# First loads reordered, blank products on TensorE at the start, and the first output tile in two transfers

## The chip, the core and the metric

The kernel runs on one NeuronCore of a Trainium2 chip. The metric is the device time of one execution in microseconds (us). A profile of one execution shows when each engine works: PE is TensorE (its weight loads are listed as PEld), DVE is VectorE, ACT is ScalarE, POOL is GpSimd, and SP only issues transfers. An issue of a transfer is listed as SPq or ACTq.

## The reference, cut to what matters

Two transformer blocks are computed for 256 tokens of width 1024, in float32. Only the first lines and the last one touch this change:

```python
# first block, start: normalise x, project it with w_in
hn = rmsnorm(h, norm_mix_g[l])
proj = jnp.einsum('bsd,de->bse', hn, w_in[l])
...
# attention of two kinds, gated FFN, then a second block with three more stages
...
# the end: the last down projection of the FFN is added to h, then normalised
h = h + swiglu(rms_norm(h, norm_ffn[layer]), ffn_w13[layer], ffn_w2[layer])
...
return rms_norm(h, final_norm)
```

## The kernel before, in words

The 256 tokens are two tiles (t = 0 and 1) of 128 tokens, one token to a partition. The width 1024 is eight chunks of 128 features. Every large product is made of three: each float32 operand is split into a high part in the type fp32r and the remainder as a low part, and PE computes high x high, low x high and high x low.

Weights come in "granules", mostly 1 MB each, through a ring of three buffers (`raw`, `w_hi`, `w_lo`). SP loads a granule into `raw`, ACT copies it to `w_hi` (line 548, for the first granule lines 624 and 627, a half each), DVE subtracts to get `w_lo` (line 1090, for the first granule line 1188, twice), and PE multiplies. Each engine has its own list of instructions, written out by hand in the order in which it executes them. Semaphores tie the lists together.

The start, engine by engine:

- SP issues x tile 0 and x tile 1 (line 400), then the first half of granule 0 of `w_in` (line 405, semaphore `first_in`), then its second half (line 406), then granules 1 and 2 (line 388), then four small transfers.
- ACT issues the identity matrix (`const`, line 613), the gain of the first norm (`norm_mix_g`, line 614) and three small vectors. It then copies the turned gain to `vcol` (line 620), converts the first half of granule 0 (line 624), then four kinds of work in turn: chunks 2 and 3 of x to `x_hi` (line 559), the second half of granule 0 (line 627), chunks 4 to 7 of x, and granule 1.
- PE waits for the identity, does two products identity x identity (`keep_busy`, line 1948, the result is not used), turns x tile 0 (line 1953, eight transposes), turns the gain (line 1979), turns x tile 1, and does two more unused products. A transpose of x tile 1 with c odd raises `xt_done`: both tiles of two chunks are then turned.
- DVE waits for `vcol` and the first `xt_done`. It writes chunks 0 and 1 of `x_hi` (line 1193), the low parts of chunks 0 to 3 (line 1102), the low parts of both halves of granule 0 (line 1188), and the low parts of chunks 4 to 7.
- PE's first real products (`first_product(0, 0)`, line 1997) need the first half of `w_hi` and the chunks of x as they come; the products with `w_lo` (line 2002) need both calls of line 1188. `first_product(1, 4)` does the same for granule 1.

The end, after the last products:

- DVE adds the product to h in four quarters (`add_last`, line 1793). ACT squares each quarter and sums it (lines 1071 and 1075, each followed by a read of the sum). DVE makes the variance (lines 1797 and 1799), POOL the inverse root (line 438), and then ACT scales the left half of a tile (`scale_half`, line 1067) and DVE the right half (`finish`, line 1808).
- Between the squares of tile 1's left half and its right half, ACT does `scale_half(0)`.
- SP sends tile 0 to `out` in one transfer after both its halves (line 424), then tile 1's right half (line 426). ACT sends tile 1's left half (line 1078).

Of the kernel before, what the change touches and what calls it, by code (L numbers as in the profile page):

```python
# [25 lines left out]
P = 128  # L26
S = 256
TT = S // P
D = 1024
# [33 lines left out]
V_MIX1, V_LB, V_CQ, V_CKV, V_END = 0, 8, 24, 26, 27  # L63
# [116 lines left out]
def build(nc, a, out):  # L180
# [9 lines left out]
    with ExitStack() as ctx:  # L190
# [10 lines left out]
        h = sb("h", [P, TT, D])  # L201
        xn = sb("xn", [P, TT, D])
# [8 lines left out]
        ps = ctx.enter_context(nc.psum_tensor("ps", [P, 8, 512], F32))  # L211
        bias_scratch = nc.dram_tensor("bias_scratch", (COPIES, HEADS, BIAS_LEN), F32, kind="Internal").ap()

        ident = const[:, K_ID:K_ID + P]


        def region(start, *dims, parts=P):
# [31 lines left out]
        bias_row = xn[0:HEADS, 1, 0:BIAS_LEN]  # L249

# [53 lines left out]
            setup warmed vrow_T vcol_done taps_T taps_done bias_ps bias_sb trig_ready  # L304
# [65 lines left out]
        def _(sp):  # L370
# [19 lines left out]
            def load_ffn(n0):  # L390
                for n in range(n0, n0 + 5):
                    load(n)
                with sp.Fori(0, 3) as i:
                    for j in range(6):
                        load(n0 + 5 + j, i, "columns" if j % 3 < 2 else "rows")
                for n in range(n0 + 23, n0 + 33):
                    load(n)

            for t in range(TT):
                sp.dma_start(h[:, t, :], a["x"][0, P * t:P * t + P, :]).then_inc(x_in[t], 16)  # L400

# [3 lines left out]
            sp.dma_start(dst[:, 0:2, :], first[:, 0:2, c0:c0 + cols]).then_inc(s["first_in"], 16)  # L405
            sp.dma_start(dst[:, 2:4, :], first[:, 2:4, c0:c0 + cols]).then_inc(raw_in[0], 16)
# [14 lines left out]
            load_ffn(G["ffn2"])  # L421
            sp.wait_ge(s["out_a"], 1)
            sp.wait_ge(s["out_b"], 1)
            sp.dma_start(out[0, 0:P, :], h[:, 0, :]).then_inc(s["out_done"], 16)
            sp.wait_ge(s["out_b"], 2)
            sp.dma_start(out[0, P:S, 512:D], h[:, 1, 512:D]).then_inc(s["out_done"], 16)
            sp.wait_ge(s["out_done"], 48)
# [110 lines left out]
        def _(act):  # L538
# [73 lines left out]
            act.activation(stat[:, 158:159], minus_half[:, 0:1], ACT.Square).then_inc(s["warmed"], 1)  # L612
            act.dma_start(const[:, K_ID:K_ID + P], a["const"][:, K_ID:K_ID + P]).then_inc(s["const_in"], 16)
            act.dma_start(vrow[V_MIX1:V_MIX1 + 8, 0, :], a["norm_mix_g"].rearrange("l (c p) -> (l c) p", p=P)).then_inc(s["mix_in"], 16)
# [6 lines left out]
            act.wait_ge(s["vcol_done"], 1)  # L621
            first_cols = 2 * granules[0][5]
            act.wait_ge(s["first_in"], 16)
            act.activation(w_hi[:, 0, 0:first_cols], raw[:, 0, 0:first_cols], ACT.Copy).then_inc(s["first_hi"], 1)
            first_operand_hi(2, 4)
# [443 lines left out]
            for t in range(TT):  # L1069
                act.wait_ge(s["last_added"], 2 * t + 1)  # L1070
                act.activation(xn[:, t, 0:512], h[:, t, 0:512], ACT.Square, accum_out=ssq_half[:, t:t + 1]).then_inc(s["half_ready"], 1)
                if t == 1:
                    scale_half(0)
                act.wait_ge(s["last_added"], 2 * t + 2)
                act.activation(xn[:, t, 512:D], h[:, t, 512:D], ACT.Square, accum_out=ssq[:, 16 + t:17 + t]).then_inc(s["ssq_ready"], 1)
            scale_half(1)
# [5 lines left out]
        def _(dve):  # L1082
# [97 lines left out]

            dve.memset(minus_half, -0.5).then_inc(s["setup"], 1)
# [643 lines left out]
        def _(pe):  # L1825
# [119 lines left out]
            def keep_busy(bank, count):  # L1945

                for _ in range(count):
                    pe.matmul(ps[:, bank, 0:P], ident, ident, start=True, stop=True)
# [25 lines left out]

            pe.wait_ge(s["const_in"], 16)
            keep_busy(7, 2)
            turn_x(0)
            pe.wait_ge(s["mix_in"], 16)
            pe.transpose(ps[:, 4, 0:8], vrow[0:8, 0, :], ident[0:8, 0:8]).then_inc(s["vrow_T"], 1)
            turn_x(1)  # L1980
            keep_busy(7, 2)
# [515 lines left out]
```

## Time and profile before

| what | value |
|---|---|
| median of three runs | 1000.36 us |
| the three runs | 999.68, 1000.36, 1000.6 us |
| the profiled execution, its own time | 999.73 us |
| span of the profiled execution, first to last instruction | 997.9 us |
| PE busy in the span | 981.6 us (98%) |
| DVE, ACT busy in the span | 677.7 us, 542.8 us |
| granted TensorE clock, mean over the span | 0.998 |

The span is 1.8 us shorter than the profiled execution's own time; what lies around it is outside the profile. The times in the rows below count from the start of the span.

### The profile page before, as it was taken

How to read it: one execution, taken by the hardware profiler on the slowest of the kernel's cores; microseconds unless marked ns; L12 is line 12 of the kernel's file. 1: busy time of each engine (PE TensorE's matmuls, PEld its weight loads, DVE VectorE, ACT ScalarE, POOL GpSimd, SP SyncE). 2: the span in 40 equal slices, each digit the busy share in tenths (PEclk: the TensorE clock that was granted, in tenths of full speed). 3: DMA queues.
4: the chain of work that ended last, by engine and by line, in shares of the span. 5: the costliest groups of instructions: out<-in, count | busy, mean ns of one | idle time of the engine just before them, and what ended most of it. 6: DMA issues, size and time to landing. Idle time of an engine off the chain costs nothing.

```text
span 997.9 us, 15646 instructions
## 1 busy us (share of the span) xinstructions
PE 981.6 (98%) x6349; PEld 841.6 (84%) x6349; DVE 677.7 (68%) x831; ACT 542.8 (54%) x708; POOL 42.9 (4%) x68
## 2 busy tenths in 40 slices
PE   7999999999999999999999999999999999999997
PEld 6887777898888888887889888888899898888885
DVE  5689787688777787777767565656656566555564
ACT  6676664476555565634445444444555455444452
POOL 1210000000000005000000000000000000000000
PEclk9999999999999999999999999999999999999999
DMA  8354335466656555844347565656553446656541
GB/s 306 103 192 158 109 120 178 161 211 211 209 170 209 171 168 164 261 146 155 120 133 259 188 207 190 204 185 201 185 168 133 155 142 214 207 172 207 174 163 43
DMA packets 121283, 175.89 MB, mean 176 GB/s; under 512 B 3167, under 2 KB 89770, under 8 KB 121226
## 3 DMA queue, kind: packets, MB, share of 16 engines
q1 hardware_dynamic: 118860, 168.82, 51.0%
q0 software_dynamic: 1600, 5.09, 1.6%
q10 hardware_dynamic: 766, 1.16, 0.5%
q8 instruction: 42, 0.69, 0.3%
q14 instruction: 15, 0.12, 0.0%
HBM read 173.82 MB, written 1.25 MB: 175 GB/s over the span
## 4 chain that ended last, share of the span: by engine, by line
PE 76%; issue 19%; DVE 2%; DMA 1%; ACT 1%; POOL 1%; SPq 0%; POOLq 0%; DVEq 0%; ACTq 0%
PE ps L1851 22%; PE ps L1901 16%; PE ps L1872 10%; PE ps L1900 7%; PE ps L1888 5%; PE ps L1915 3%; PE ps L1923 2%; DMA raw<-in_w_in 1%; PE ps L2141 1%; PE ps L2336 1%; PE ps L1903 1%; PE ps L1966 1%; PE ps L2169 1%; PE ps L2397 1%; PE ps L1997 1%
## 5 line engine op out<-in xcount | busy, mean ns | idle before, releaser
L1090 DVE TENSOR_TENSOR w_lo<-raw,w_hi 128x2048 fp32r<-128x2048 f32 (+3 forms) x153 | 345.3, 2261 | 125.2 <-ACT w_hi L548 124.9
L1901 PE MATMUL ps<-x_both,w_hi 128*128 128x512 f32 x992 | 342.7, 396 | 0.0
L548 ACT ACTIVATE w_hi<-raw 128x2048 fp32r<-128x2048 f32 (+3 forms) x161 | 302.4, 1879 | 58.9 <-PE ps L1851 40.1
L1900 PE MATMUL ps<-x_both,w_lo 128*128 128x256 f32 x868 | 242.0, 279 | 0.0
L1901 PEld LDWEIGHTS ps<-x_both,w_hi 128*128 128x128 f32 x992 | 179.1, 188 | 34.5
L1900 PEld LDWEIGHTS ps<-x_both,w_lo 128*128 128x128 f32 x868 | 163.6, 189 | 5.5
L803 ACT ACTIVATE work<-ps 128x512 f32<-128x512 f32 x66 | 39.3, 596 | 150.2 <-PE ps L1901 134.4
L1851 PE MATMUL ps<-w_hi,x_both 128*128 128x512 f32 (+1 forms) x320 | 101.5, 387 | 0.3 <-DVE w_lo L1090 0.3
L1851 PE MATMUL ps<-w_hi,hid_hi 128*128 128x512 f32 x240 | 93.8, 391 | 0.0
L1851 PE MATMUL ps<-w_hi,hid_lo 128*128 128x512 f32 x240 | 93.4, 389 | 0.0
L1851 PE MATMUL ps<-w_lo,hid_hi 128*128 128x512 f32 x240 | 93.4, 389 | 0.0
L1498 DVE TENSOR_TENSOR work<-ps,work 128x512 f32<-128x512 f32 x66 | 45.5, 689 | 63.1 <-ACT work L803 62.8
L1872 PE MATMUL ps<-w_hi,x_both 128*128 128x512 f32 x256 | 84.3, 398 | 0.1
L1851 PEld LDWEIGHTS ps<-w_hi,x_both 128*128 128x128 f32 x320 | 59.2, 188 | 13.0 <-issue 1.9
L1851 PE MATMUL ps<-w_lo,x_both 128*128 128x512 f32 (+1 forms) x160 | 60.7, 379 | 0.0
L837 ACT ACTIVATE hid_hi<-work 128x512 fp32r<-128x512 f32 x33 | 20.8, 631 | 68.9 <-DVE work L1530 62.7
L1872 PEld LDWEIGHTS ps<-w_hi,x_both 128*128 128x128 f32 x256 | 48.1, 188 | 10.4 <-DVE w_lo L1090 0.5
L1851 PEld LDWEIGHTS ps<-w_hi,hid_lo 128*128 128x128 f32 x240 | 45.0, 188 | 9.5
L1851 PEld LDWEIGHTS ps<-w_lo,hid_hi 128*128 128x128 f32 x240 | 45.1, 188 | 9.4
L1851 PEld LDWEIGHTS ps<-w_hi,hid_hi 128*128 128x128 f32 x240 | 45.1, 188 | 8.2
L1915 PE MATMUL ps<-x_both,w_hi 128*128 128x256 f32 x384 | 49.4, 284 | 1.5 <-DVE x_both L1109 1.5
L1872 PE MATMUL ps<-w_lo,x_both 128*128 128x512 f32 x128 | 49.9, 390 | 0.0
(294 smaller groups left out, 1274.2 us busy)
## 6 DMA issues: line engine op xcount, KB each, us to landing
raw<-in_ffn_w SPq DMA_DIRECT2D x66, 1024.0 KB, 5.1
raw<-in_w_up SPq DMA_DIRECT2D x22, 1024.0 KB, 5.1
raw<-in_hgrn_w_in SPq DMA_DIRECT2D x16, 1024.0 KB, 5.5
raw<-in_w_in SPq DMA_DIRECT2D x12, 1024.0 KB, 5.2
raw<-in_moba_w_in SPq DMA_DIRECT2D x12, 1024.0 KB, 5.2
raw<-in_w_down SPq DMA_DIRECT2D x11, 1024.0 KB, 5.0
raw<-in_w_out SPq DMA_DIRECT2D x4, 1024.0 KB, 5.1
raw<-in_hgrn_w_out SPq DMA_DIRECT2D x4, 1024.0 KB, 5.7
```

The costliest lines, as they stand in the source:

```text
L548: act.activation(w_hi[:, n % RING, 0:kc * cols], raw[:, n % RING, 0:kc * cols], ACT.Copy).then_inc(s["hi_ready"], 1)
L803: act.activation(up[:, p % 2, 2 * half:2 * half + 2, :], src[:, :, S:2 * S], ACT.Copy).then_inc(s["up_half"], 1)
L837: act.activation(hid_hi[:, 2 * par:2 * par + 2, :].rearrange("p a b -> p (a b)"), hid[:, par, :], ACT.Copy).then_inc(s["hhi_ready"], 1)
L1090: dve.tensor_tensor(w_lo[:, n % RING, sl], raw[:, n % RING, sl], f32(w_hi[:, n % RING, sl]), ALU.subtract).then_inc(s["lo_ready"], 1)
L1498: dve.tensor_tensor(v, src[:, :, 0:S], v, ALU.add).then_inc(s["up_taken"], 1)
L1851: ins = pe.matmul(ps[:, bank + 2 * c + t, 0:n_c], x[:, chunks + kk, P * t:P * t + P], w[:, n % RING, w0:w0 + n_c], start=(first and kk == ...
L1872: ins = pe.matmul(ps[:, bank + 2 * c + t, :], x[:, chunks + kk, P * t:P * t + P], w[:, n % RING, w0:w0 + 512], start=(first and kk == 0 an ...
L1888: ins = pe.matmul(ps[:, bank, S * f:S * f + S], w[:, n % RING, 256 * k + P * f:256 * k + P * f + P], x[:, k, :], start=(k == 0 and q == 0) ...
L1900: pe.matmul(out[:, 0, :], w_lo[:, n % RING, at], x_hi[:, k, :], start=False, stop=False)
L1901: ins = pe.matmul(out, w_hi[:, n % RING, at], x_both[:, k, :, :], start=(k == 0), stop=(k == DC - 1))
L1915: pe.matmul(out[:, :, at_t], w_hi[:, n % RING, 256 * k + P * f:256 * k + P * f + P], x_both[:, k, :, at_t], start=(k == 0 and t == 0), sto ...
L1923: ins = pe.matmul(ps[:, banks[f], 0:S], w_lo[:, n % RING, 256 * k + P * f:256 * k + P * f + P], x_hi[:, k, :], start=False, stop=(k == DC ...
```

## The change

Five edits, all at the two ends of the kernel:

1. SP loads x tile 1 after the first half of granule 0 and no longer ahead of it.
2. ACT issues the gain ahead of the identity. Its wait for its own `vcol` comes after the conversion of granule 0's first half.
3. DVE first writes zeros into 128 columns of `xn` (`blank`), and PE multiplies this blank with itself eight times as its first work. PE then waits for identity and gain, turns the gain ahead of x tile 0, and does four unused products identity x identity between the two tiles of x. The two after x tile 1 stay.
4. ACT's `scale_half(0)` comes after both squares of tile 1.
5. SP sends the right half of tile 0 as soon as it is scaled, and the left half in a second transfer.

```diff
--- before.py
+++ after.py
@@ -247,6 +247,7 @@
         pool_tmp = region(13776, 4, 160 * TT)
         g_ik = region(16592, HD)
         bias_row = xn[0:HEADS, 1, 0:BIAS_LEN]
+        blank = xn[:, 0, 0:P]
 
 
         conv = region(0, 2, 4, S)
@@ -301,7 +302,7 @@
         table = sb("table", [NBUCKET + 1, HEADS])
 
         names = """small_in mix_in first_in first_hi first_lo gate_scale first_x taps_in pos_in posrow_in const_in shapes_in gain_in table_in masks_in final_in final2_in bias_out bias_in out_done
-            setup warmed vrow_T vcol_done taps_T taps_done bias_ps bias_sb trig_ready
+            setup blank warmed vrow_T vcol_done taps_T taps_done bias_ps bias_sb trig_ready
             hi_ready lo_ready products_done
             ssq_ready var_ready rstd_ready  xt_done xhi_ready xlo_ready h_added scaled_done h_final last_added half_scaled half_ready out_a out_b
             row_ready half_turned half_hi half_lo grow_in last_gate og_part og_scaled f_half f_sum q_half q_sum
@@ -396,13 +397,16 @@
                 for n in range(n0 + 23, n0 + 33):
                     load(n)
 
-            for t in range(TT):
+            def load_x(t):
                 sp.dma_start(h[:, t, :], a["x"][0, P * t:P * t + P, :]).then_inc(x_in[t], 16)
+
+            load_x(0)
 
             first = a["w_in"][0].rearrange("(c p) n -> p c n", p=P)
             dst, cols = granule_views(0)
             c0 = granules[0][4]
             sp.dma_start(dst[:, 0:2, :], first[:, 0:2, c0:c0 + cols]).then_inc(s["first_in"], 16)
+            load_x(1)
             sp.dma_start(dst[:, 2:4, :], first[:, 2:4, c0:c0 + cols]).then_inc(raw_in[0], 16)
             for n in range(1, RING):
                 load(n)
@@ -419,12 +423,13 @@
             for n in range(G["mq"], G["ffn2"]):
                 load(n)
             load_ffn(G["ffn2"])
+            sp.wait_ge(s["out_b"], 1)
+            sp.dma_start(out[0, 0:P, 512:D], h[:, 0, 512:D]).then_inc(s["out_done"], 16)
             sp.wait_ge(s["out_a"], 1)
-            sp.wait_ge(s["out_b"], 1)
-            sp.dma_start(out[0, 0:P, :], h[:, 0, :]).then_inc(s["out_done"], 16)
+            sp.dma_start(out[0, 0:P, 0:512], h[:, 0, 0:512]).then_inc(s["out_done"], 16)
             sp.wait_ge(s["out_b"], 2)
             sp.dma_start(out[0, P:S, 512:D], h[:, 1, 512:D]).then_inc(s["out_done"], 16)
-            sp.wait_ge(s["out_done"], 48)
+            sp.wait_ge(s["out_done"], 64)
 
 
         @block.gpsimd
@@ -610,18 +615,18 @@
 
             act.wait_ge(s["setup"], 1)
             act.activation(stat[:, 158:159], minus_half[:, 0:1], ACT.Square).then_inc(s["warmed"], 1)
+            act.dma_start(vrow[V_MIX1:V_MIX1 + 8, 0, :], a["norm_mix_g"].rearrange("l (c p) -> (l c) p", p=P)).then_inc(s["mix_in"], 16)
             act.dma_start(const[:, K_ID:K_ID + P], a["const"][:, K_ID:K_ID + P]).then_inc(s["const_in"], 16)
-            act.dma_start(vrow[V_MIX1:V_MIX1 + 8, 0, :], a["norm_mix_g"].rearrange("l (c p) -> (l c) p", p=P)).then_inc(s["mix_in"], 16)
             for r, name in ((V_LB, "hgrn_lb_logits_2"), (V_CQ, "q_a_norm_g"), (V_CKV, "kv_a_norm_g")):
                 v = a[name]
                 v = v.rearrange("l (c p) -> (l c) p", p=P)
                 act.dma_start(vrow[r:r + v.shape[0], 0, :], v).then_inc(s["small_in"], 16)
             act.wait_ge(s["vrow_T"], 1)
             act.activation(vcol[:, 0, 0:8], ps[:, 4, 0:8], ACT.Copy).then_inc(s["vcol_done"], 1)
-            act.wait_ge(s["vcol_done"], 1)
             first_cols = 2 * granules[0][5]
             act.wait_ge(s["first_in"], 16)
             act.activation(w_hi[:, 0, 0:first_cols], raw[:, 0, 0:first_cols], ACT.Copy).then_inc(s["first_hi"], 1)
+            act.wait_ge(s["vcol_done"], 1)
             first_operand_hi(2, 4)
             act.wait_ge(raw_in[0], 16)
             act.activation(w_hi[:, 0, first_cols:2 * first_cols], raw[:, 0, first_cols:2 * first_cols], ACT.Copy).then_inc(s["hi_ready"], 1)
@@ -1069,10 +1074,9 @@
             for t in range(TT):
                 act.wait_ge(s["last_added"], 2 * t + 1)
                 act.activation(xn[:, t, 0:512], h[:, t, 0:512], ACT.Square, accum_out=ssq_half[:, t:t + 1]).then_inc(s["half_ready"], 1)
-                if t == 1:
-                    scale_half(0)
                 act.wait_ge(s["last_added"], 2 * t + 2)
                 act.activation(xn[:, t, 512:D], h[:, t, 512:D], ACT.Square, accum_out=ssq[:, 16 + t:17 + t]).then_inc(s["ssq_ready"], 1)
+            scale_half(0)
             scale_half(1)
             act.wait_ge(s["out_a"], 2)
             act.dma_start(out[0, P:S, 0:512], h[:, 1, 0:512]).then_inc(s["out_done"], 16)
@@ -1178,6 +1182,7 @@
                         add(t, c, 4 + 2 * c + t)
                 return adds
 
+            dve.memset(blank, 0.0).then_inc(s["blank"], 1)
             dve.memset(minus_half, -0.5).then_inc(s["setup"], 1)
             dve.memset(table[NBUCKET:NBUCKET + 1, :], -FAR).then_inc(s["setup"], 1)
             first_cols = 2 * granules[0][5]
@@ -1942,10 +1947,10 @@
                     feature_high(n + g, banks[g], 1, ready if g == 0 else None)
                     feature_low(n + g, banks[g])
 
-            def keep_busy(bank, count):
+            def keep_busy(bank, count, operand):
 
                 for _ in range(count):
-                    pe.matmul(ps[:, bank, 0:P], ident, ident, start=True, stop=True)
+                    pe.matmul(ps[:, bank, 0:P], operand, operand, start=True, stop=True)
 
             def turn_x(t):
                 pe.wait_ge(x_in[t], 16)
@@ -1972,13 +1977,15 @@
                         pe.wait_ge(s["half_lo"], step(k, t, c // 4))
                 return ready
 
+            pe.wait_ge(s["blank"], 1)
+            keep_busy(7, 8, blank)
             pe.wait_ge(s["const_in"], 16)
-            keep_busy(7, 2)
-            turn_x(0)
             pe.wait_ge(s["mix_in"], 16)
             pe.transpose(ps[:, 4, 0:8], vrow[0:8, 0, :], ident[0:8, 0:8]).then_inc(s["vrow_T"], 1)
+            turn_x(0)
+            keep_busy(7, 4, ident)
             turn_x(1)
-            keep_busy(7, 2)
+            keep_busy(7, 2, ident)
             def in_block(b, k):
                 token_product(2 * b + k, 4 * k, 4 + 2 * (b % 2), k == 0, k == 1)
```

## Rows read from the trace of the kernel before

**Rows 1.** The page: busy time, share of the span and instructions of each engine.

```profile
PE 981.6 (98%) x6349; PEld 841.6 (84%) x6349; DVE 677.7 (68%) x831; ACT 542.8 (54%) x708; POOL 42.9 (4%) x68
```

**Rows 2.** Busy time by stretch, PE alone: stretch, length, PE busy, granted clock, DMA share, GB/s.

```profile
20.97:984.00 963.03, 958.89 (x6247) 1.00 0.53 175
991.07:997.93 6.86, 0.00 (x0) 0.74 0.39 153
```

**Rows 3.** The chain that ended last, 0 to 25 us: start, length, what.

```profile
1.20 0.42 SPq L400
...
1.66 7.11 DMA raw<-in_w_in
...
8.86 1.02 ACT w_hi L624
...
9.93 3.82 PE ps L1997 x16
...
15.79 3.58 PE ps L1997 x16
```

**Rows 4.** Timeline of PE's weight loads: start, length, instructions, idle before and releaser.

```profile
4.87 0.93 PEld L1948 LDWEIGHTS ps<-const 128*128 128x128 f32 x4 [4.87 <-DMA const<-in_const]
5.68 1.72 PEld L1953 LDWEIGHTS ps<-const,h 128*128 128x128 f32 x8
...
7.93 0.86 PEld L1953 LDWEIGHTS ps<-const,h 128*128 128x128 f32 x8
...
13.74 1.63 PEld L2002 LDWEIGHTS ps<-w_lo,x_both 128*128 128x128 f32 x8 [0.40 <-DVE w_lo L1188]
```

**Rows 5.** DMA issues of the first 3 us: size and us from issue to landing.

```profile
const<-in_const ACTq DMA_DIRECT2D x1, 64.0 KB, 3.9
...
h<-in_x SPq DMA_DIRECT2D x1, 512.0 KB, 4.9
raw<-in_w_in SPq DMA_DIRECT2D x1, 488.0 KB, 7.1
...
raw<-in_w_in SPq DMA_DIRECT2D x1, 488.0 KB, 7.8
```

**Rows 6.** DMA queues from 5.5 to 7 us: packets, MB, share of 16 engines.

```profile
q0 software_dynamic: 32, 0.00, 41.4%
```

**Rows 7.** Timeline of the start, DVE.

```profile
8.50 0.88 DVE L1193 TENSOR_SCALAR x_both<-ps,vcol 128x256 fp32r<-128x256 f32 x2 [7.49 <-PE ps L1953]
...
10.64 0.88 DVE L1102 SCALAR_TENSOR_TENSOR x_both<-ps,vcol,x_both 128x256 fp32r<-128x256 f32 x2 [0.49 <-ACT x_both L559]
11.44 2.25 DVE L1188 TENSOR_TENSOR w_lo<-raw,w_hi 128x976 fp32r<-128x976 f32 x2
```

**Rows 8.** Timeline of the start, transfers issued by ACT and SP.

```profile
1.36 0.57 ACTq L614 DMA_DIRECT2D work<-in_norm_mix_g  x1
...
2.13 0.68 SPq L406 DMA_DIRECT2D raw<-in_w_in  x1
```

**Rows 9.** Timeline of the end, after the last product.

```profile
991.21 0.68 DVE L1793 TENSOR_TENSOR h<-ps,h 128x512 f32<-128x512 f32 x1
991.73 0.72 ACT L1067 ACTIVATE h<-work,stat 128x512 f32<-128x512 f32 x1 [0.54 <-POOL stat L438]
...
992.36 0.61 ACT L1075 ACTIVATE xn<-h 128x512 f32<-128x512 f32 x1
...
992.88 0.19 ACT L1075 ACTIVATION_READ_ACCUMULATOR xn<-h 128x1 f32 x1
993.17 0.16 DVE L1799 SCALAR_TENSOR_TENSOR stat<-stat 128x1 f32<-128x1 f32 x1 [0.55 <-ACT xn L1075]
993.40 0.55 POOL L438 TENSOR_TENSOR stat<-stat 128x1 f32<-128x1 f32 x1 [1.71 <-DVE stat L1799]
...
993.99 0.75 DVE L1808 SCALAR_TENSOR_TENSOR h<-h,stat,g_final 128x512 f32<-128x512 f32 x1 [0.66 <-POOL stat L438]
...
994.77 0.36 SPq L426 DMA_DIRECT2D out<-h  x1
```

**Rows 10.** The tile out, its three transfers: us from issue to landing.

```profile
DMA to landing us min/median/max: 2.6/2.6/2.8
```

## The prediction

> **What bounds the kernel now.** I read the page's busy times first. PE is busy 981.6 us [rows 1] of a span of 997.9 us, so only 16.3 us are left in which PE does nothing. The busy times by stretch show where they are: between 20.97 and 984.00 PE lacks 963.03 - 958.89 = 4.1 us [rows 2], and after its last product at 991.07 come 6.86 us without it. The rest is the start: 4.87 us before the first product and about half a microsecond before 9.93. The change edits nothing between 21 and 991 us. It can move the time by what it does to the moment at which PE gets through granule 0, and by what it does to the 6.86 us of the end. A measurement of this kernel can tell about 0.2%, 2.0 us, from no change.
>
> The chain of waits shows what releases the first real product: the transfer of granule 0's first half, issued at 1.66 and 7.11 us on its way (1.66 + 7.11 = 8.77), then its conversion from 8.86 for 1.02 us, then the products at 9.93 [rows 3]. The reader should also see the next piece: these 16 products take 3.82 us, the same 16 for granule 1 take 3.58 (0.224 each). The difference of 0.24 us is a second wait: PE's loads of `w_lo` begin at 13.74 after 0.40 idle, released by DVE's line 1188 [rows 4]. So a second chain ends almost with the first, and it is DVE's: it begins at 8.50 when the second tile of x has been turned, holds one wait of 0.49 us (for ACT's chunks 2 and 3), and ends at 11.44 + 2.25 = 13.69 [rows 7]. Without the wait it is 13.69 - 8.50 - 0.49 = 4.70 us of work. Whatever the change does to the first chain, PE cannot leave granule 0 before the second has ended.
>
> **Edit 1, the order of the loads.** x tile 1 was issued at 1.20 [rows 3] and landed 4.9 us later [rows 5], at 6.1; the half granule behind it landed at 8.77. The two swap places in one queue and are nearly of one size (512 and 488 KB). The half granule should land near 6.1 and its conversion end near 7.2, 2.7 us earlier than now. x tile 1 then lands in the place of the half granule. Call that moment T1. Bounds: not before 6.1 plus the time of 488 KB at about 400 GB/s (the spacing of two later 488 KB landings, 8.77 and 2.13 + 7.8 = 9.93 [rows 5, 8], is 1.16 us), so 7.3; and not much after the landing now in that place, 8.8, with 9.1 as outer end. What speaks for the late end is the stretch from 5.5 to 7 us, in which GpSimd's small transfers hold 41.4% of the 16 DMA engines while moving next to nothing [rows 6]. They are issued when they were, so what is in flight then is slowed, and that is now x tile 1. I take 8.7.
>
> Now DVE's chain starts from T1. PE turned tile 1 from 7.93 [rows 4] and DVE began at 8.50, 0.57 later. With T1 = 8.7 DVE begins at 9.27. The wait of 0.49 goes away: ACT has long converted the first half granule and is free for chunks 2 and 3 at once. DVE ends at 9.27 + 4.70 = 13.97, PE starts `w_lo` 0.05 later as now, at 14.02 against 13.74: 0.28 us lost. PE's own side is earlier: eight transposes of x tile 1 (1.1 us) and four passes of unused products (0.43) let it start at about 10.2, and 16 products of 0.224 end at 13.8. The start of real products moves back by about 0.3 as well, though its old releaser, the half granule, came 2.7 us sooner. In this sum the transfer moved ahead buys nothing, because the one moved behind now ends both chains. By T1's bounds the term is 7.3 + 5.32 - 13.74 = -1.1 us to 9.1 + 5.32 - 13.74 = +0.7 us. At the low end the second half of granule 0 (landing 9.93, conversion 1.02, then eight products of 0.224 after it: 12.8) limits it to -0.9.
>
> **Edit 2, gain ahead of identity.** The gain's issue takes 0.57 us [rows 8] and the zeroing ahead about 0.1 (bounds 0.05 and 0.5, by a 128-partition copy of 256 columns, half of 0.88 us in [rows 7]), so the identity, which takes 3.9 us from issue [rows 5] and starts PE at 4.87 [rows 4], lands about 0.65 us later, near 5.5. Turning the gain and x tile 0 takes about 0.2 + 0.86 at the fast pitch or 0.2 + 1.72 at the slow one [rows 4]: done by 7.5 at the latest, over a microsecond before T1. The cover is the wait for x tile 1. If x tile 1 came at 7.3, the slow case would cost 0.2 us.
>
> **Edit 3, blank products.** The row of x tile 0's loads shows 8 in 1.72 us, 0.215 each; tile 1's are 8 in 0.86, 0.107 each [rows 4]. Same instruction, half the time: PE ran at the lower of its two levels (1.2 GHz) until about 7.9 and at 2.4 GHz after it, three microseconds after its first product at 4.87. The granted clock is not recorded as low there; the pitch is what shows it. Eight blanks are 16 passes of about 0.2 us, 3.3 us from about 1.1 to 4.4. They lie in time in which PE waited. If the clock rises as it did, x tile 0 is turned 0.9 us quicker, behind the cover of edit 2, so this is worth nothing here. The four products between the tiles (eight passes, 0.86 us) end near 7.5, also under cover. Then PE has nothing for about 1.2 us until T1. The profile shows PE with nothing from 991.07 and the granted clock at half only late in that stretch: 0.74 as mean over 6.86 us is half speed for 3.6 us, so it fell 3.3 us after the last product [rows 2]. From 20.97 to 984 us it is 1.00 although PE's gaps there sum to 4.1 us. No row shows it falling in a gap as short as 1.2, so I leave it at 2.4 GHz. The Trainium skill (TensorE: Matmul & The Clock Gate, Part 1) says that the throttled clock is the default, that activity releases it, and that the moment of the rise varies from run to run of one kernel. The trace agrees with the first two by the pitches 0.215 and 0.107; one execution can't show the third. By it the runs above 999.73 could be ones with a late rise, and blanks would take this away: a rival below.
>
> **Edits 4 and 5, the end.** ACT scales tile 0 from 991.73 for 0.72 and squares tile 1's last quarter only from 992.36 [rows 9]. The quarter is there at 991.21 + 0.68 = 991.89. Squared first, it starts at about 991.93, 0.43 earlier, and the sum's read (992.88), the variance (993.17), the root (993.40) and the last scaling (993.99) each waited for the one before: all move by 0.43. The scaling of tile 0 then runs at about 992.56 to 993.28, before ACT is wanted again at 993.56. SP issues tile 0's left half at 993.3 in 0.36 us and is free at 993.7; the right half of tile 1 is ready at 994.31. So nothing is queued in front, and the last issues move from 994.77 to 994.34. Each output transfer lands 2.6 to 2.8 us after issue [rows 10]. Splitting tile 0 adds one transfer ahead of the last pair. Bounds: nothing, or, if its data ran into theirs, 256 KB at 400 GB/s, 0.65 us. It is issued 1.0 us before them, so I take nothing. The Trainium skill (DMA: Bandwidth & Descriptors, Rules for kernel authors) advises one large transfer over several small ones; by it the split could only cost, up to those 0.65 us. No row shows such an output pair side by side other than tile 1's, which lands in the same 2.6 to 2.8 us.
>
> **Sum.** +0.28 (start) - 0.43 (end) = -0.15 us against the profiled execution's 999.73: 999.6. The median of the runs shown is 0.63 above it; carried there the forecast is 1000.2. I give 1000.0, between the two.
>
> **Rivals.** (a) x tile 1 lands early, because the slow stretch belongs to the half granule's short rows and not to the clock time: start -0.9, end -0.43, time 998.4 to 999.0. For it: the 488 KB took 2.7 us behind x tile 1, the next 488 KB only 1.16. Against it: [rows 6]. (b) Other side: the clock is down when x tile 1 comes, because eight blanks stop at 4.4 and the two gaps (4.4 to 5.5, 7.5 to 8.7) keep it low or let it fall. Transposes and the unused passes then take 1.72 + 0.8 us, real products begin at 11.3 at 0.448 each, and if the rise comes 3.0 us after T1 as it did after 4.87, `w_lo` starts at about 15.1: +1.4, net +1.0, time 1000.7 to 1001.3. It is slower by over 0.2% only if half speed lasts past 13.9 (11.3 + 3.58 + half of 2.6 gives 16.2 for `w_lo`, 2.4 after 13.74, which is 2.0 with the end's gain). (c) Blanks remove a late rise that the slower of the three runs had: about 999.2. (d) The end gives nothing, since the split or ACT's order brings another wait: 1000.4. For it: four engines hand over within 3 us there. Against: each wait in [rows 9] names the one before.
>
> **Chances.** Forecast 0.57, (a) 0.13, (b) 0.12, (c) 0.09, (d) 0.09. Nearly all of this lies within 2 us of 1000.36. Faster by over 0.2% needs (a) and (c) together: 0.05. Slower needs (b) with a long slow stretch: 0.04. Same 0.91. The range 998.6 to 1001.3 leaves out the low end of (a) and the high end of (b), about 1.5 in 10.
>
> **What would show it.** After the change: line 405's half granule landing near 6.1 and x tile 1's near 8.7; DVE's line 1193 starting 0.57 after that, without a wait of 0.49 before its third pair of low parts; PE's `w_lo` products starting near 14.0; loads of x tile 0 at a pitch of 0.107; the last square starting 0.04 after the last add, and the last two issues about 3.1 us after that add's start, not 3.56. Wrong: x tile 1 before 8 us or after 9; a pitch of 0.215 for x tile 1; the end shortened by less than 0.3 us, or the stretch from 21 to 984 us changed by over 0.5 us, which nothing here explains.

## The result, and the profile after

The changed kernel takes 1003.3 us in the median of seven runs (1002.82 to 1003.95), the kernel before 1000.05 beside it: ratio 1.0033, interval 1.0023 to 1.0042. It is slower by 3.3 us; 1000.0 was forecast, with 1001.3 as upper end.

The page after, its first lines:

```profile
span 1001.1 us, 15688 instructions
...
PE 986.7 (99%) x6369; PEld 846.9 (85%) x6369; DVE 677.8 (68%) x832; ACT 542.8 (54%) x708; POOL 42.9 (4%) x68
```

PE is busy 5.1 us more than in [rows 1], and the span is 3.2 longer. It is not a new idle stretch that shows, but more work on PE, or the same at a slower pitch. The chain that ended last, 0 to 25 us, of the changed kernel (start, length, what; its line 1958 is the old 1953, 1953 the old 1948, 2004 and 2009 the old 1997 and 2002):

```profile
1.73 6.51 DMA const<-in_const
...
8.29 0.27 PE ps L1984
8.56 1.90 PE ps L1958 x8
10.46 1.71 PE ps L1953 x8
12.17 1.63 PE ps L1958 x8
13.80 0.45 PE ps L1953 x4
14.24 3.56 PE ps L2004 x16
17.80 1.77 PE ps L2009 x8
```

In [rows 3] a transfer of weights began this chain. Now it is the identity: issued at 1.73, it is 6.51 us on its way. From there PE has no gap: gain, x tile 0, the four unused products, x tile 1, the last two, and the real products at 14.2. The landings of the first transfers (size, us from issue to landing) and the timeline of PE's weight loads:

```profile
const<-in_const ACTq DMA_DIRECT2D x1, 64.0 KB, 6.5
...
h<-in_x SPq DMA_DIRECT2D x1, 512.0 KB, 7.3
...
raw<-in_w_in SPq DMA_DIRECT2D x1, 488.0 KB, 4.5
```

```profile
1.07 3.49 PEld L1953 LDWEIGHTS ps<-xn 128*128 128x128 f32 x16 [1.07 <-DVE xn L1185]
8.29 0.18 PEld L1984 LDWEIGHTS ps<-const,work 8*128 8x128 f32 x1 [3.73 <-DMA const<-in_const]
8.49 1.57 PEld L1958 LDWEIGHTS ps<-const,h 128*128 128x128 f32 x8
10.04 1.83 PEld L1953 LDWEIGHTS ps<-const 128*128 128x128 f32 x8
11.75 1.72 PEld L1958 LDWEIGHTS ps<-const,h 128*128 128x128 f32 x8
13.45 0.60 PEld L1953 LDWEIGHTS ps<-const 128*128 128x128 f32 x4
```

The order of the loads did what was forecast: the half granule landed at 1.20 + 4.5 = 5.7, x tile 1 at 1.66 + 7.3 = 8.96. But PE asks for x tile 1 only at 11.75. The blanks end at 4.56, and for 3.73 us PE has nothing. After that both tiles of x go at the slow pitch: 1.72 / 8 = 0.215, where x tile 1 in [rows 4] went at 0.107. Last, the end (timeline, after the last product):

```profile
994.83 0.68 DVE L1798 TENSOR_TENSOR h<-ps,h 128x512 f32<-128x512 f32 x1
...
995.54 0.63 ACT L1078 ACTIVATE xn<-h 128x512 f32<-128x512 f32 x1 [0.73 <-DVE h L1798]
...
996.17 0.71 ACT L1072 ACTIVATE h<-work,stat 128x512 f32<-128x512 f32 x1
...
996.37 0.16 DVE L1804 SCALAR_TENSOR_TENSOR stat<-stat 128x1 f32<-128x1 f32 x1
996.61 0.55 POOL L443 TENSOR_TENSOR stat<-stat 128x1 f32<-128x1 f32 x1 [1.29 <-DVE stat L1804]
...
997.19 0.75 DVE L1813 SCALAR_TENSOR_TENSOR h<-h,stat,g_final 128x512 f32<-128x512 f32 x1 [0.67 <-POOL stat L443]
```

From the last add to the last scaling it is 997.19 - 994.83 = 2.36 us, against 993.99 - 991.21 = 2.78 in [rows 9]: 0.42 gained, 0.43 forecast.

**Where 3.2 us went.** The products with `w_lo` begin on the chain at 17.80 instead of 13.75: +4.05. Of it 8.29 - 4.87 = 3.42 is the later identity, 0.63 what follows it. The end gives -0.4. In the middle, between 424 and 478 us, the waits of PE that the profile calls "issue" (time in which PE waited for nothing that the profile shows) are 0.5 in place of 1.3 us: -0.8 (below). PE's loads for the turning of `xn` wait 0.4 us more between 75 and 248 us. The sum is +3.25, the spans differ by 3.2.

### The profile page after: what moved, and what is told of

It is laid out like the page before. It is cut to its first block, busy times and chain, and to the rows that moved or that the text cites. A ratio compares the mean times of both kernels' runs of the same rounds, so it can differ in the third digit from the quotient of the medians.

```text
span 1001.1 us, 15688 instructions
## 1 busy us (share of the span) xinstructions
PE 986.7 (99%) x6369; PEld 846.9 (85%) x6369; DVE 677.8 (68%) x832; ACT 542.8 (54%) x708; POOL 42.9 (4%) x68
## 4 chain that ended last, share of the span: by engine, by line
PE 76%; issue 19%; DVE 2%; DMA 1%; ACT 1%; POOL 1%; POOLq 0%; DVEq 0%
PE ps L1856 22%; PE ps L1906 16%; PE ps L1877 10%; PE ps L1905 7%; PE ps L1893 5%; PE ps L1920 3%; PE ps L1928 2%; PE ps L2148 1%; PE ps L2343 1%; PE ps L1908 1%; PE ps L1971 1%; PE ps L2176 1%; PE ps L2404 1%; PE ps L2004 1%; PE ps L2167 1%
## 5 line engine op out<-in xcount | busy, mean ns | idle before, releaser
L1856 PEld LDWEIGHTS ps<-w_hi,x_both 128*128 128x128 f32 x320 | 59.2, 188 | 13.1 <-issue 2.0
```

The lines of the kernel that those rows point to most:

```text
L1856: ins = pe.matmul(ps[:, bank + 2 * c + t, 0:n_c], x[:, chunks + kk, P * t:P * t + P], w[:, n % RING, w0:w0 + n_c], start=(first and kk == ...
```

## The experiments

The table has every run: median of 10 or 11 executions (the first two rows: seven), their lowest and highest, ratio to the kernel before with its 95% interval, and from the profiled execution the landing of the identity, the start of PE's `w_lo` loads of granule 0, and PE's waits for "issue" in the middle, all at one line: that of the small products of one attention (line 2336 in the kernel before). The kernel before ran at 999.96 to 1000.19 beside them.

| kernel | median (range) us | ratio (interval) | identity | `w_lo` | issue |
|---|---|---|---|---|---|
| before | 1000.05 (999.68-1000.6) | 1 | 4.87 | 13.74 | 1.3 |
| changed | 1003.3 (1002.82-1003.95) | 1.0033 (1.0023-1.0042) | 8.24 | 17.42 | 0.5 |
| e1 identity first | 1000.42 (999.49-1000.97) | 1.0005 (0.9996-1.0014) | 5.0 | 14.33 | 0.8 |
| e2 gain first alone | 1000.65 (1000.1-1002.71) | 1.0007 (0.9998-1.0016) | 7.56 | 16.85 | 1.1 |
| e3 no four | 1002.74 (1000.06-1003.65) | 1.0025 (1.0016-1.0035) | 8.58 | 16.01 | 0.7 |
| e4 end alone | 999.43 (999.15-1000.06) | 0.9995 (0.9986-1.0004) | 4.7 | 13.92 | 0.8 |
| e5 small late | 1001.69 (1000.78-1003.18) | 1.0020 (1.0011-1.0029) | 6.85 | 16.31 | none |
| e6 blanks long | 1000.41 (999.73-1000.9) | 1.0002 (0.9993-1.0011) | 7.5 | 15.34 | 0.2 |
| e7 loads alone | 1001.29 (999.77-1002.3) | 1.0012 (1.0003-1.0021) | 4.95 | 15.78 | 1.1 |
| e8 blanks alone | 999.89 (999.28-1001.28) | 1.0003 (0.9994-1.0012) | 4.8 | 14.27 | 0.4 |
| e9 best | 997.76 (997.32-999.01) | 0.9980 (0.9971-0.9989) | 4.6 | 12.67 | 0.4 |
| e10 small late alone | 999.35 (999.01-1000.02) | 0.9995 (0.9986-1.0004) | 4.79 | 13.80 | 1.5 |
| e11 changed, mended | 999.01 (998.16-999.96) | 0.9990 (0.9981-0.9999) | 4.8 | 13.52 | 0.8 |
| e12 best, no blanks | 999.14 (998.53-1001.26) | 0.9994 (0.9985-1.0003) | 4.8 | 13.52 | 1.5 |
| f1 identity first, 14 blanks | 998.65 (998.39-999.43) | 0.9985 (0.9976-0.9995) | 5.0 | 14.56 | none |
| f2 gain first, 20 blanks | 1000.26 (999.82-1000.89) | 1.0001 (0.9992-1.0010) | 8.1 | 15.06 | none |
| f3 loads, 14 blanks | 998.98 (998.55-999.84) | 0.9989 (0.9980-0.9999) | 4.9 | 14.64 | none |
| g1 waits only | 999.77 (998.46-1001.69) | 0.9996 (0.9987-1.0005) | 4.8 | 14.05 | 1.0 |
| g2 best + waits | 998.82 (997.18-999.99) | 0.9984 (0.9975-0.9993) | 4.9 | 13.54 | 1.1 |
| g3 14 blanks alone | 998.6 (998.25-999.1) | 0.9988 (0.9979-0.9997) | 4.8 | 13.73 | none |

**The order of ACT's issues (e1, e2).**

```diff
 # e1, on the changed kernel: the identity ahead of the gain again
-act.dma_start(vrow[V_MIX1...]).then_inc(s["mix_in"], 16)
 act.dma_start(const[:, K_ID:K_ID + P], ...).then_inc(s["const_in"], 16)
+act.dma_start(vrow[V_MIX1...]).then_inc(s["mix_in"], 16)
 # e2, on the kernel before: the same two lines swapped, gain first, nothing else
```

> The changed kernel with ACT's first two issues in the old order, identity ahead of gain. Theory Q (the identity, issued second, has its last packets in the stretch in which GpSimd's small transfers hold the DMA engines, and everything on PE waits for it): the identity lands at 4.9 to 5.2 instead of 8.24, PE's first transposes start near 5.2, x tile 1 (8.96) is waited for, real products start at 10.4 to 11.8 instead of 14.0, time 1000.1 to 1001.3. Rival L (the order of the x and weight loads sets the loss): stays at 1002.8 to 1003.5.

> The kernel before with nothing but ACT's first two issues swapped, gain ahead of identity. Theory Q: the identity lands about 3 us later than 4.87, PE begins near 8, all transposes at the slow pitch of 0.215, real products near 13.5, time 1003.0 to 1003.8. If the swap alone is worth only its 0.6 us of issue time (my prediction's step): identity near 5.5, time 1000.0 to 1000.7.

e1 gives back 2.9 of 3.3 us, so without the late identity there is no such loss. It took the slow pitch away as well: in its profiled execution both tiles of x are turned at 0.107 (the row is shown with e11 below), so e1 does not part the two. Its chain of waits (start, length, what):

```profile
1.66 7.40 DMA h<-in_x
...
12.11 2.18 DVE w_lo L1193 x2
...
14.33 2.05 PE ps L2009 x8
```

It is the chain of my prediction: x tile 1 lands at 9.06 and the products with `w_lo` start 5.27 us later (5.32 forecast). With the swap alone (e2) the profiled execution has the identity 6.00 us on its way and takes 1002.71, but 8 of 11 executions take 1000.1 to 1000.7. So the swap does not always bring the late landing, and my expectation of 1003.0 to 1003.8 missed. Only profiled executions show the landing; that the fast ones had it early is argued, not shown.

**The four unused products (e3).** The line `keep_busy(7, 4, ident)` is taken out of the changed kernel.

> The changed kernel without the four unused products between the two tiles of x. Theory C (they run at the slow clock on the path once the identity is late): 8 passes of 0.23, so 1.8 us less, 1001.3 to 1001.7. If the clock rises a fixed time after PE begins: the rest runs slow for longer, and only part comes back, 1001.7 to 1002.5. If x tile 1 or DVE's chain sets the start, nothing changes: 1003.2.

0.6 us less in the median, so the median missed all three of my cases; the executions go from 1000.06 to 1003.65, where the changed kernel never went below 1002.82. The eight passes took 1.7 us on the chain after, so taking them out moves the rest forward but not by all of it each time. The profiled execution (`w_lo` at 16.01 instead of 17.42) also records the clock. Busy time by stretch, PE alone (stretch, length, PE busy, granted clock, DMA share, GB/s):

```profile
1.07:5.00 3.93, 3.78 (x16) 1.00 0.79 266
5.20:8.50 3.30, 0.00 (x0) 1.00 0.93 241
8.60:11.90 3.30, 3.27 (x16) 0.50 1.05 406
12.00:18.00 6.00, 6.00 (x32) 1.00 0.59 183
```

After a stretch without work on PE the granted clock is half from 8.6 to 11.9, where both tiles of x are turned, and full from 12. The 1.00 of the first row is not full speed: the 16 loads of the blanks take 3.48 us there, 0.22 each. As in [rows 4], a slow start is not recorded as such, and the pitch has to show it. So a fall of the clock is recorded here; in the profiled execution of the changed kernel none is, and whether the clock fell there in the gap or had never risen stays open. The blanks had been done for four microseconds when the work that they were to serve began.

**The end alone (e4).** Edits 4 and 5 on the kernel before, as in the diff of the change.

> The kernel before with the two edits of the end alone (scaling of tile 0 after both squares, tile 0 out in two transfers). By the prediction's sum: 0.43 us less, 999.6. Rival (d), another wait takes its place: 1000.0 to 1000.4.

999.43, 0.6 less; the interval (0.9986 to 1.0004) holds both no change and the 0.43 of the sum. The profile after has the 0.42 row by row.

**GpSimd's small transfers (e5, e10).**

```diff
 # e5, on the changed kernel; e10, on the kernel before, with first_in in place of const_in
+pool.wait_ge(s["const_in"], 16)
 pool.dma_start(pos_i[:, :], ...).then_inc(s["pos_in"], 16)
 pool.dma_start(table[0:NBUCKET, :], ...).then_inc(s["table_in"], 16)
```

> The changed kernel with GpSimd's two small transfers (positions and bias table) issued only once the identity has landed; nothing else changed. Theory Q (their slow packets hold the engines on which the identity's last packets wait): the identity, still issued second, lands at 5.0 to 5.8, x tile 1 at 7.4 to 8.0 instead of 8.96, time 999.3 to 1000.8 depending on the clock. Rival S (being second on ACT's queue behind the gain is slow by itself, or the queue of the weights holds it up): the identity still lands at 7.5 to 8.6, time 1002.5 to 1003.5.

> The kernel before with GpSimd's two small transfers issued only after the first half granule has landed, nothing else. Theory Q: the half granule lands near 7.7 instead of 8.77. Then PE's transposes at the slow pitch and DVE's chain behind them set the start: x tile 1 turned from about 7.8 as now, DVE from 8.5, so the products with the low part near 13.3: 999.4 to 999.7, about 0.5 less. If the blanks have no part in the gain of the best kernel: 998.2 to 998.6.

In e5 the identity takes 5.1 us instead of 6.5 and x tile 1 6.2 instead of 7.3. Issued second with GpSimd's transfers in flight, the identity took 5.8 to 6.8 us in five profiled executions (the changed kernel, e2, e3, e6, f2), so these transfers make 0.7 to 1.7 us of its lateness. The rest of the way from 3.9 [rows 5] goes with its later place, and my landing at 5.0 to 5.8 was too early. The median falls by 1.6 us, to above the range that I gave. e10 moves the half granule's landing from 8.77 to 1.66 + 5.7 = 7.4, and the `w_lo` loads stay at 13.80. It is not the prediction's second chain that holds them: DVE has `w_lo` ready at 11.03 + 2.25 = 13.28, and PE's loads wait for nothing:

```profile
7.85 1.57 PEld L1954 LDWEIGHTS ps<-const,h 128*128 128x128 f32 x8
9.40 0.98 PEld L1949 LDWEIGHTS ps<-const 128*128 128x128 f32 x4
10.26 3.50 PEld L1998 LDWEIGHTS ps<-w_hi,x_both 128*128 128x128 f32 x16
13.80 1.73 PEld L2003 LDWEIGHTS ps<-w_lo,x_both 128*128 128x128 f32 x8
```

PE's own work, without a gap from the identity on, sets them. The prediction had PE's side too, but only at the fast pitch, where it ends before DVE's; x tile 1 goes here in 1.57 us instead of 0.86 [rows 4], and the unused products in 0.98 instead of 0.53. e12 starts its `w_lo` loads at 13.52 in the same way.

**The clock (e6, e8).** `keep_busy(7, 20, blank)` in place of 8 in the changed kernel (e6); the eight blanks ahead of the kernel before with no other edit (e8).

> The changed kernel with 20 blank products instead of 8, so that PE works until about 7.3 to 9. The identity stays late (about 8.2). Theory C (the other half of the loss is that everything after the identity, four unused products among it, runs at the slow clock, because the eight blanks end at 4.6 and 3.7 us without work follow): transposes at the pitch of 0.107 after the identity, real products from about 11.5 instead of 14.0, time 1000.9 to 1001.7. If the clock has no part in it: 1003.0 to 1003.5.

> The kernel before with the eight blank products in front alone. My prediction's step (worth nothing, since it lies under the wait for the half granule) gives 1000.0. If the earlier clock frees DVE's chain: the products with the low part start about 0.2 us sooner and runs with a late rise of the clock go away, 999.6 to 999.9. If the blanks end too early and the clock falls back as the real work starts: 1000.3 to 1001.5.

PE's weight loads in e6:

```profile
1.06 7.00 PEld L1953 LDWEIGHTS ps<-xn 128*128 128x128 f32 x40 [1.06 <-DVE xn L1185]
8.19 0.13 PEld L1984 LDWEIGHTS ps<-const,work 8*128 8x128 f32 x1
8.34 0.85 PEld L1958 LDWEIGHTS ps<-const,h 128*128 128x128 f32 x8
...
15.34 1.62 PEld L2009 LDWEIGHTS ps<-w_lo,x_both 128*128 128x128 f32 x8 [0.55 <-DVE w_lo L1193]
```

The identity is used no sooner than at 8.19, but x is turned at 0.106 each and the `w_lo` loads start at 15.34 instead of 17.42. Time 1000.41: again 2.9 us back, and under my range.

This is the experiment that parts clock and identity, and the start of the `w_lo` loads gives the shares, each from one profiled execution: 13.74 before; 14.33 with the new order of loads alone in the way (e1), +0.6; 15.34 with the late identity as well (e6), +1.0; 17.42 with the slow pitch as well, +2.1. So the largest part of the loss is work at the slow pitch that the late identity has put on the critical chain. The times of e6 and f2 hide what the late identity costs by itself: their `w_lo` loads start 1.6 and 1.3 us later than before, and 1.0 us comes back in the middle in both (below), in e6 another 0.4 at the end.

e8 is unchanged in the median, with 4 of 11 executions at 1000.87 to 1001.28; its profiled execution has the half granule 7.65 us on its way in place of 7.11. The granted clock, as a mean over the span, is 0.996 or 0.997 in those four and 0.998 or 0.999 in the other seven. So those four ran some us more at half clock, as in rival (b); where these lie no trace shows.

**The order of the loads (e7, f1, f3), and gain first with the clock up (f2).** e7 has edit 1 alone; f3 the same with 14 blanks; f1 is the changed kernel with the identity first and 14 blanks; f2 is e2 with 20 blanks.

> The kernel before with the order of SP's first loads alone changed (x tile 1 behind the first half granule). My prediction's step: x tile 1 lands near 9.0, DVE's chain starts 0.57 to 0.7 later and the products with the low part start 5.3 after the landing, near 14.3 instead of 13.74: 1000.4 to 1000.8. If the identity is pushed back as well or the clock falls in the gap before x tile 1: 1001 or more. If the order is hidden: 1000.0.

> The changed kernel with the identity ahead of the gain and 14 blank products instead of 8, so that PE has no gap before the identity is used. If order of loads is all that is left: x tile 1 near 9.0, products with the low part near 14.3, all at the fast pitch, 1000.0 to 1000.4 with little spread (e1: 999.49 to 1000.97). If the late identity was costless in e6 (1000.41) too: the same as e6 within 0.2.

> The kernel before with gain ahead of identity and 20 blank products in front. If the clock makes most of the swap's cost in its slow executions (1001.8 to 1002.7 in e2): none above 1001.2, median 1000.2 to 1000.9, real products from about 10.5 in place of 13.1. If the late identity alone makes it: executions above 1001.8 remain.

> The kernel before with the changed order of loads and 14 blank products in front. Prediction's chain with the clock up: x tile 1 near 9.0, products with the low part 5.3 later at 14.3, so 0.6 more than before: 1000.4 to 1000.8, against 1001.29 without the blanks. If the order costs by something besides x tile 1's landing and the clock: 1001.0 or more.

e7 is 1.3 us slower than before. x tile 1 lands at 9.02, and PE, which had nothing for 1.08 us, turns it at 0.2 each; the `w_lo` loads start at 15.78, where the prediction's sum (9.02 + 5.32) has 14.34. With the clock up, f1 and f3 have x tile 1 at 9.29 and 9.37 and `w_lo` at 14.56 and 14.64, 5.27 later in both. f2 has no execution above 1000.89 where e2 has three above 1001.7. All this is as the clock theory says. But f1 and f3 are 1.4 and 1.1 us faster than the kernel before, which ran at 1000.1 beside them, where I expected no gain or a loss. The start is 0.8 and 0.9 later in them; the time comes back elsewhere.

**What the time comes back from (g1, g2, g3).** Waits of PE between 380 and 480 us, in the kernel before (who waited for what: total, times, longest):

```profile
PE ps L2336 <- issue: 1.3, 1, 1.3
PE ps L1915 <- DVE x_both L1109: 0.8, 1, 0.8
PE ps L1966 <- DVE xn L1621: 0.3, 1, 0.3
```

and in g3:

```profile
PE ps L1917 <- DVE x_both L1110: 0.8, 1, 0.8
PE ps L1968 <- DVE xn L1623: 0.2, 1, 0.2
```

Line 2336 has rows of 128 products of 32 columns, and one last row of 64. In the kernel before, the stretch from 400 to 500 us has 1320 products, the other full hundreds from 100 to 900 us 526 to 670. The wait stands inside the row of 64 (the chain that ended last, the kernel before, then g3):

```profile
470.34 1.03 PE ps L2336 x57
471.37 1.29 issue
472.66 0.32 PE ps L2336 x7
472.98 2.94 PE ps L1872 x12
```

```profile
470.37 1.14 PE ps L2340 x64
471.50 2.94 PE ps L1874 x12
```

At this row the two executions are within 0.03 us of each other; behind it g3 is 1.48 us ahead. Between 424 and 474 us eight loads of instructions, 0.13 MB, run in the kernel before; from 471 to 473 us no transfer of any kind runs. That PE waits for its instructions here is argued below, not shown. g1 has 56 fulfilled waits ahead of PE's first instruction (the trace has 28 instructions for them), g2 24 ahead of the best kernel's blanks (12 instructions), g3 14 blanks alone:

```diff
 # g1
+for _ in range(56):
+    pe.wait_ge(s["setup"], 1)
 pe.wait_ge(s["const_in"], 16)
 # g3
+pe.wait_ge(s["blank"], 1)
+keep_busy(7, 14, blank)
 pe.wait_ge(s["const_in"], 16)
```

> The kernel before with 56 waits in front of PE's first instruction, all fulfilled after the first microsecond, in time in which PE has nothing to do until 4.87; no other edit. If the place of PE's instructions in its code decides the wait near 471 us: that wait of 1.3 us goes or shrinks, the start stays (products with the low part at 13.7), 998.6 to 999.3. If it was the blanks or the clock: 1000.0 to 1000.2.

> The best kernel (end edits, eight blanks, GpSimd's transfers late) with 24 fulfilled waits more in front on PE. By the code's place: the stretch from 424 to 474 us becomes 0.6 us shorter, as in f1 and f3, 997.1 to 997.4. If it has no such part: 997.76.

> The kernel before with 14 blank products in front, nothing else. If the order of loads costs what the chain says (0.5 to 0.9 us, by x tile 1's late landing), this is faster than f3 (998.98) by that: 998.1 to 998.5. If the order is free once the clock is up: 998.9 to 999.1. If PE's number of instructions ahead sets the stretch from 424 to 474 us: that stretch is near 47.9 us as in f3 and f1, against 48.5 with eight blanks and 49.3 with none; else near 49.

(DVE's zeroing of `blank` is left out of the cut of g3.) g3 is 998.6, and its `w_lo` loads start at 13.73, to 0.01 where they start before. Nothing of its gain is at the start; its span is 1.5 us shorter and the wait of 1.3 is gone. By number of added products at the start the wait is 0.8 to 1.5 with none, 0.7 and 0.8 with 6, 0.4 with 8, none to 0.8 with 10, none with 14, 16 and 20, 0.2 with 22. Added waits don't follow this: g1 has 1.0, and g2, the best kernel plus 12 instructions, went from 0.4 to 1.1. g2's blanks also started at 2.34 instead of 1.06, a transfer of constants costs it 0.5 us near 27 us, and it is 1.1 us slower than e9. In time neither decides: g1's median lies between its two cases, g2's above both.

The place of the wait does follow a rule. Count how many of the 64 products stand before it. With nothing added it is 57 (before, e2, e4, e7, e10, e12); with 26 more instructions in the trace 44 (e3, e11), with 28, all of them semaphore instructions, 43 (g1), with 33 41 (e8, e9), with 42 36 (e1 and the changed kernel), with 45 35 (g2). A product with its load is two instructions, so the wait moves ahead in the row by half of what was added: it stands at one place in the count of instructions, whatever was added and at whatever time PE gets there. With 57 and more added (g3, f3, f1, f2, e6) no wait is left in this row, where the rule would put it after 28 products or fewer; in e6 a short one stands in an earlier row. So what was added moves the place, and a border between loaded blocks of instructions would behave like this. How long the wait is does not follow: with 42 it is 0.8 in e1, none in e5, and 0.2 there and 0.3 in an earlier row in the changed kernel.

g3 against f3 gives the price of the load order with the clock up: 998.98 - 998.6 = 0.4 us, and the intervals of the two overlap nearly whole; in the profiled executions `w_lo` starts 0.9 later.

**The best version (e9, e11, e12).** e9 is the kernel before with edits 4 and 5, eight blanks, and GpSimd's two transfers held until the first half granule has landed. e12 is e9 without the blanks. e11 is the changed kernel with the identity first, without the four products, and with GpSimd's transfers held until x tile 1 has landed.

> The kernel before with the two edits of the end, the eight blanks in front, and GpSimd's two small transfers issued only after the first half granule has landed. Theory Q: without them the half granule lands near 7.6 instead of 8.77, real products start near 8.8 and those with the low part near 12.7 instead of 13.74, time 998.3 to 998.9. If the slow stretch from 5.5 to 7 us is not GpSimd's doing: 999.4 as with the end's edits alone.

> The changed kernel with identity ahead of gain, without the four unused products, and with GpSimd's two small transfers issued after x tile 1 has landed; the changed order of SP's loads stays. By x tile 1's landing near 7.8 plus 5.3, the products with the low part start near 13.1: 998.2 to 998.9. If the order of loads costs by itself against the best kernel (12.67): 0.4 us slower than it, 998.2; if not, 997.8.

> The best kernel without the eight blank products: end edits and GpSimd's late transfers only. If the blanks matter once GpSimd's transfers are out of the way (turning x at the fast pitch lets DVE's chain start near 7.2 instead of 8.5): 998.8 to 999.3, about 1.2 slower than 997.76. If they do not: 997.7 to 998.1.

The chain of e9:

```profile
1.66 6.04 DMA raw<-in_w_in
...
7.79 1.02 ACT w_hi L627
...
8.86 3.82 PE ps L2002 x16
12.68 2.03 PE ps L2007 x8
```

The half granule lands at 7.70 instead of 8.77, the blanks run until the identity is there, and real products start at 8.86 instead of 9.93. 997.76 is 2.2 us under the kernel before: 1.07 at the start, 0.4 at the end, and the rest in the middle, with a wait of 0.4 instead of 1.3. That last part is why it came out under the 998.3 to 998.9 that I expected. Without blanks (e12) the `w_lo` loads start at 13.52, 0.85 later, and the time is 1.4 more; the wait in the middle is 1.5 there, so the blanks' gain is not only the clock's.

e11, at 999.01, is just above my range, with `w_lo` at 13.52 instead of near 13.1. x tile 1 landed as expected, at 7.8, but its eight blanks did not bring the fast pitch. PE's loads of x tile 0, in e1 and in e11, both after eight blanks that end at 4.5 to 4.6:

```profile
5.86 0.85 PEld L1958 LDWEIGHTS ps<-const,h 128*128 128x128 f32 x8
```

```profile
6.05 1.57 PEld L1959 LDWEIGHTS ps<-const,h 128*128 128x128 f32 x8
```

The gap after the blanks is 1.2 us in e1 and 1.3 in e11, and the pitch is 0.106 in one and 0.2 in the other. Eight blanks raised the clock in time in some executions (e1, e9) and not in others (e11). With 14 or 20 blanks x is turned at the fast pitch in all five profiled executions (e6, f1, f2, f3, g3).

## Why the prediction was wrong

- **Edit 2 failed first.** "The identity [...] lands about 0.65 us later, near 5.5" was worked from the issue time alone, with the way of 3.9 us kept. Its issue came 0.8 us later (1.73 instead of 0.93), and it took 6.5: PE used it at 8.29 instead of 4.87. I had set GpSimd's slow stretch [rows 6] against x tile 1 and not against the identity, which the swap moves toward it. Held off, these transfers give 0.7 to 1.7 us back (e5); the rest is not taken apart.
- **Edit 3 failed with it.** "I leave it at 2.4 GHz": that was for a gap of 1.2 us, and the gap was 3.73. Rival (b) had this mechanism (work at half pitch after blanks that end too early), with the wrong gap, so its price of 1.0 us was too small. By e6 the slow pitch makes 2.1 us of the later start. The rows show half clock after the gap in e3. In e1, whose two gaps are 1.0 and 1.26 us, x tile 1 is turned at 0.107, and there "no fall in a gap as short as 1.2" held. But that the clock rises behind eight blanks at all, "as it did", was taken from one execution: in e11 it had not risen after them, with a gap of 1.3. In e7, with no blanks ahead, the pitch is slow throughout.
- **Edit 3's cover was gone.** The four unused products were costed at nothing, "under cover" of the wait for x tile 1. With the identity at 8.24 there is no such wait, and they lie on the chain with 1.71 us.
- **Edit 1's mechanism was right.** x tile 1 landed at 8.96 (8.7 taken, 8.8 and 9.1 as upper bounds), and in e1, f1 and f3 the `w_lo` products started 5.27 us after it. The moved transfer buys nothing. It costs 0.4 us with the clock up, which is not clear of the noise, and 1.3 without blanks. What the sum lacked is PE's own side at the slow pitch, where it ends later than DVE's chain (e7, e10); only rival (b) had it. In the changed kernel itself the term was hidden behind the identity.
- **The end was right**, 0.42 us by the rows for 0.43.
- **The 21 to 984 us** were taken as untouched. They gave 0.4 us back, for the two reasons in the account above; why the wait for "issue" got shorter is open.
- On the Trainium skill's sentence that the moment of the rise varies from run to run (TensorE: Matmul & The Clock Gate, Part 1): the trace agrees. In the kernel before, e4, e10, e12 and g1 PE begins with the same products at 4.7 to 4.9; the eight loads of x tile 1 take 0.86 us in the kernel before and 1.57 in the other four. So one execution could not show it, and rival (c) had a true premise. That eight blanks take the late rise away is not borne out (e8, e11).

## What to carry to other kernels

Reorder first loads only with the landing times of all of them in view: a small transfer that everything waits for should be issued first, because its way can grow by far more than the issue slot it loses, and slow small transfers of another engine that aren't needed yet should wait. Unused products that are to hold the clock up should be enough in number and reach until the real work starts: 14 and 20 did so in every profile here, eight did not; and unused products behind an uncertain wait are a cost when that wait moves. Where two causes are tied together, as late identity and slow pitch here, one run that keeps the first and takes away only the second (e6) says more than one that takes away both (e1). Before a gain at the start is explained by the start, compare where the real products begin: in g3 they begin as before, and the gain comes more than 400 us later.

## What the runs showed that was not expected

- The place of PE's instructions matters. A wait of 1.3 us in a row of 64 products of 32 columns, for no engine and no transfer that the profile shows, went with 14 unused products added more than 400 us ahead (998.6 against 1000.04 beside it). In all 14 profiled executions that have the wait in this row it stands at one place in the count of PE's instructions; semaphore instructions move it like products. What sets its length stays open: 28 added semaphore instructions left it at 1.0, and with the same ten added products it was 0.5, 0.8 and none in three profiled executions.
- GpSimd's two transfers of 1 KB each hold 41.4% of the DMA engines' time from 5.5 to 7 us [rows 6]; with them held back, nothing of this queue is left in that stretch and 488 KB of weights land 1.1 us sooner (e9) and 1.4 with no other edit (e10), at a cost of one wait.
